# Seams of a two-stream transformer kernel: last chunks multiplied tile by tile, no context rows inside, and modulation pieces in places of their own

## The reference, cut to what matters

```python
def first_block(x, c, ...):
    c_act = jax.nn.silu(c)
    for l in range(DEPTH):                                  # 2
        mod = c_act @ w_ada[l] + b_ada[l]                   # 1024 -> 6 rows of 1024
        sh_m, sc_m, gt_m, sh_f, sc_f, gt_f = jnp.split(mod[:, None, :], N_MOD, axis=-1)
        h = rms_norm(x, g_pre_mix[l]) * (1.0 + sc_m) + sh_m
        y = token_mixer(h, w_in[l], ..., w_out[l], cos, sin)   # w_in 1024 x 3656, attention, w_out 1024 x 1024
        x = x + gt_m * rms_norm(y, g_post_mix[l])
        h = rms_norm(x, g_pre_ffn[l]) * (1.0 + sc_f) + sh_f
        y = conv_glu_ffn(h, w_up_act[l], w_up_lin[l], w_conv[l], b_conv[l], w_down[l])  # 2 x 2816 up, 2816 down
        x = x + gt_f * rms_norm(y, g_post_ffn[l])
    return x

def second_block(x, c, ctx, c_ctx, ...):
    for i in range(DEPTH):                                  # layer 0 even, layer 1 odd
        yc, yl = even_mixer(...) if i % 2 == 0 else odd_mixer(...)
        ...
        ff = peer(...)                                      # context and latents in layer 0, latents in layer 1
    return rmsnorm(hl, norm_f_g)

def peer(h, w_q, subkeys, u, v):                            # per token: 8 heads x 16 experts of 16384
    q = (xb @ w_q).reshape(PEER_BLOCK, PEER_HEADS, 2, PEER_DHALF)
    ...                                                     # top 16 of each half, then top 16 of 256 sums
    ue, ve = u[idx], v[idx]
    act = jax.nn.gelu(jnp.einsum('td,thkd->thk', xb, ue), approximate=False)
    return jnp.einsum('thk,thkd->td', g * act, ve)
```

## Time and profile before

| | us |
|---|---|
| median of three timed runs | 3843.72 |
| lowest and highest of them | 3842.69 and 3852.66 |
| the profiled execution's own time | 3842.15 |
| its span, first to last instruction | 3840.9 |
| TensorE busy in the span | 3050.1 (79%) |
| VectorE busy | 2455.0 (64%) |
| ScalarE, GpSimd busy | 784.2 (20%), 940.7 (24%) |
| moved by DMA | 1102.15 MB, mean 287 GB/s |

### The profile page before, as it was taken

The page is one execution under the profiler, slowest core; times in us unless marked ns, Lnnn a source line. Parts: engine busy times, 40 slices in busy tenths (PEclk is TensorE's granted clock), DMA queues, the critical chain, the costliest instruction groups (busy, mean ns, idle before and its releaser), DMA issues. The chain is left out here.

```text
span 3840.9 us, 28366 instructions
## 1 busy us (share of the span) xinstructions
PE 3050.1 (79%) x8769; PEld 1590.1 (41%) x8769; DVE 2455.0 (64%) x5374; ACT 784.2 (20%) x1876; POOL 940.7 (24%) x842
## 2 busy tenths in 40 slices
PE   6898797899786799787767777777897787777776
PEld 1354464675334377254344223322343462233322
DVE  3224556887677488646656999766514519999665
ACT  1102223232224433225211111100102211111000
POOL 0000001222221233222302344434100013444432
PEclk7999898999898899888879998999996799999999
DMA  6654234999795689966847999999632059999998
GB/s 236 201 178 167 93 114 169 343 356 354 301 356 199 230 349 406 373 248 212 306 154 294 391 388 389 392 422 422 257 138 103 21 206 367 386 389 376 422 421 348
DMA packets 194025, 1102.15 MB, mean 287 GB/s; under 512 B 22517, under 2 KB 22849, under 8 KB 95569
## 3 DMA queue, kind: packets, MB, share of 16 engines
q0 software_dynamic: 114512, 818.87, 54.1%
q1 hardware_dynamic: 78736, 280.90, 20.2%
q10 hardware_dynamic: 624, 0.57, 0.1%
HBM read 1099.18 MB, written 1.05 MB: 286 GB/s over the span
## 5 line engine op out<-in xcount | busy, mean ns | idle before, releaser
L2022 PE MATMUL PS<-AR 128*128 128x512 f32 x2464 | 1216.7, 639 | 400.7 <-DVE AR L2064 341.2
L2121 POOL DMA_INDIRECT AR<-in_uv,AR x768 | 866.1, 1128 | 1641.9 <-PE PS L2022 1142.8
L2069 DVE CUSTOM_DVE_ANT_0 AR<-AR 128x1024 f32<-128x1024 f32 x768 | 935.6, 1220 | 297.2 <-DMA AR<-in_uv,AR 296.7
L2022 PEld LDWEIGHTS PS<-AR 128*128 128x128 f32 x2464 | 476.1, 202 | 1103.3 <-DVE AR L2064 536.5
L694 PE MATMUL PS<-AR 128*128 128x512 f32 (+3 forms) x1304 | 565.3, 588 | 27.4 <-DMA AR<-in_w_in 14.7
L2034 ACT ACTIVATE AR<-AR 128x2 f32<-128x2 f32 x384 | 78.1, 203 | 1514.8 <-DVE AR L2069 1509.2
L694 PEld LDWEIGHTS PS<-AR 128*128 128x128 f32 x1304 | 250.5, 205 | 314.9 <-issue 269.5
L991 PE MATMUL PS<-AR 128*128 128x256 f32 x1408 | 327.2, 392 | 22.9 <-DMA AR<-in_w_up_act 11.9
L326 DVE SCALAR_TENSOR_TENSOR AR<-AR,CC 128x512 f32<-128x512 f32 x280 | 210.5, 752 | 208.5 <-DMA AR<-in_w_ada 130.7
L991 PEld LDWEIGHTS PS<-AR 128*128 128x128 f32 x1408 | 273.2, 196 | 85.0 <-issue 17.4
L1941 PE MATMUL PS<-AR 128*128 128x256 f32 x768 | 186.7, 406 | 26.7 <-DMA AR<-in_peer_w_q 19.6
(11 more groups left out here) (226 smaller groups left out, 2490.3 us busy)
## 6 DMA issues: line engine op xcount, KB each, us to landing
AR<-in_w_mod SPq DMA_DIRECT2D x96, 512.0 KB, 4.3
AR<-in_w_ada SPq DMA_DIRECT2D x96, 512.0 KB, 4.6
AR<-in_w_in SPq DMA_DIRECT2D x56, 512.0 KB, 4.0
AR<-in_peer_w_q SPq DMA_DIRECT2D x48, 512.0 KB, 3.3
AR<-in_w_up_act SPq DMA_DIRECT2D x44, 512.0 KB, 7.7
AR<-in_w_up_lin SPq DMA_DIRECT2D x44, 512.0 KB, 7.5
AR<-in_w_down SPq DMA_DIRECT2D x44, 512.0 KB, 9.6
AR<-in_even_w_in SPq DMA_DIRECT2D x24, 512.0 KB, 4.2
```

The costliest lines, as they stand in the source:

```text
L2022: ins = pe.eng.matmul(acc[i][hh], e.dg(x), e.buf(x)[:, 1024 + 512 * hh:1536 + 512 * hh], start=(x == e.on[False][i][0]), stop=(x == e.on[F ...
L2069: v.eng.tensor_tensor_reduce(e.buf(x)[:, 0:1024], e.buf(x)[:, 0:1024], norm2(e).H[e.tiles[x // 128]], 1.0, 0.0, ALU.mult, ALU.add, DT[x // ...
L2121: g.eng.indirect_dma_start(e.buf(x), None, D["uv"][e.l], bass.IndirectOffsetOnAxis(ap=idx_at(x // 16, x % 16, 1), axis=0)).then_inc(*land. ...
```

## The change

The last column block of a linear layer at a seam (w_out and w_down of layer 1, w_down of layer 0, the even mixer's output) is no longer multiplied chunk by chunk with tile 0 and tile 1 in turn: its four chunks are held in the ring, all of tile 0 is multiplied, then all of tile 1. The first column block after a norm (w_in of layer 1, the even mixer's input) is done in the same way. The epilogue (squares, root, gated add) is written for one tile at a time, and a dummy square root is put ahead of it. The shares at the seams (1.5 and 2.0) become 0, and the even mixer's shares are multiplied by 1.5. Modulation pieces of three sets (`ada0b`, `ada1a`, `ada1b`) go in halves of 256 KB into three places of their own instead of into the ring; in layer 1 they start four chunks later. Which context rows VectorE sums is moved by 8 to 11 rows. In the latents' query stages the top-k search starts at step 3 instead of 11, with four units instead of one, and the first no longer waits for the modulation rows, whose sums have moved out of its work area.

The diff, cut to its core:

```diff
@@ places and Mods @@
+        OWN_T = [T[:, a:a + 512] for a in (1536, 3072, 3584)]
+        OWN_BIG = [BIG[:, 5632 + 512 * i:6144 + 512 * i] for i in range(3)]
+        ACM = [area("acc")[:, 512 * i:512 * i + 512] for i in range(2)]
@@ Mods.sp @@
+                place, n = {}, len(self.own)
                 for j, hh, outs in self.halves:
                     r = 2 * j + hh
                     for kh in range(4):
-                        load(sp, ("raw", self.key, j, hh, kh), self.w[r, kh].rearrange("p (c n) -> p c n", c=2),
-                             2, 512, [("piece", self.key, j, hh, kh)])
+                        if n:
+                            for c in range(2):
+                                i = self.nth(j, hh, kh, c) % n
+                                sp.wait_ge(place.get(i, self.guard))
+                                sp.eng.dma_start(self.own[i], self.w[r, kh, :, 512 * c:512 * c + 512]).then_inc(
+                                    *land.landed(f"own{i}", "raw", self.key, j, hh, kh, c))
+                                place[i] = ("piece", self.key, j, hh, kh, c)
+                        else:
+                            load(sp, ...)
                         yield
@@ lin_pe @@
+                if c0 in whole:
+                    if k0 == 0:
+                        held = [(k, *chunk(pe, block(w, nk, c0, n, k, kk), kk, n, False)) for k in range(0, nk, kk)]
+                    if k0 // kk < len(tiles):
+                        t = tiles[k0 // kk]
+                        if t not in seen:
+                            prep.prep(pe, t)
+                            seen[t] = prep.turned(t)
+                        pe.wait_ge(seen.get(t))
+                        for ka, k, wt in held:
+                            pe.wait_ge(("raw", k))
+                            for kc in range(kk):
+                                ins = pe.eng.matmul(bks[k0 // kk][:, 0:n], lhs(ka + kc, t), wt[:, kc, :],
+                                                    start=(ka + kc == 0), stop=(ka + kc == nk - 1))
...
+                    yield
+                    continue
@@ lin @@
+                if c0 in whole:
+                    made = None
+                    if 0 <= k0 // kk - 2 < len(tiles):
+                        take(lane, tiles[k0 // kk - 2], c0, n)
@@ first block @@
+        HEAD, TAIL = ((), (0,)), ((), (512,))
-        CH, ROW, PACE, ATT = 0.45, 0.47, 0.8, (1.2, 0.5)
+        CH, ROW, PACE, ATT, SEAM = 0.45, 0.47, 0.8, (1.2, 0.5), 0.0
@@ first_pe, w_in (and the same loop condition in first_sp, first_act, first_dve, first_pool) @@
+            for i, _ in enumerate(lin_pe(pe, ("win", l), ..., ring=FIRST[l], whole=HEAD[l])):
+                if i >= 4 * len(HEAD[l]):
+                    pe.fill()
                 yield CH
@@ first_pe, w_out and the norm ahead of the FFN @@
-            yield 1.5
+            yield SEAM
             pe.run(mods_of["next", l])
             for t in range(2):
                 n2.prep(pe, t)
+            yield 1.0
             pe.wait_ge([n2.turned(t) for t in range(2)])
-            yield 1.0
@@ first_pe, w_down @@
             for f in range(22):
+                if f == 18:
+                    held = [(x, *chunk(pe, wd[:, x:x + 1, :], 1, 1024, False)) for x in range(18, 22)]
+                for x, k, wt in held if f in (18, 19) else ():
+                    pe.wait_ge(("raw", k), ("glu", l, x))
+                    down(x, k, wt, f - 18)
+                if f < 18:
+                    ...
                 yield CH
-            yield 2.0
+            yield SEAM
@@ first_act (first_dve and first_pool have add_dve and add_pool for tile f - 20 at the same f) @@
+            for f in range(22):
+                if f == 18:
+                    a.wait_ge(a.last)
+                    a.eng.activation(dum, dum, ACT.Sqrt).then_inc(*a.done())
+                if f >= 20:
+                    for hh in range(2):
+                        take_y(a, ("y", ("ffn", l)), f - 20, hh, ("mm", "y", ("ffn", l), f - 20))
+                    rms_y(a, l, 3, f - 20)
+                yield CH
+            yield SEAM
@@ even mixer, latent side @@
+                            whole=(0,) if side == "l" else ()):        # ein
+                            whole=(512,) if side == "l" else ()):      # eout
@@ who uses what @@
-                mods_of["first", 0] = ada("ada0b", 0, (2, 4, 3, 5), AF, {0: n1r, 1: n1r}, n1t)
+                mods_of["first", 0] = ada("ada0b", 0, (2, 4, 3, 5), AF, {0: n1r, 1: n1r}, n1t, OWN_T)
@@ (mods_of["first", 1] takes OWN_T too, mods_of["next", 0] takes OWN_BIG; more takes ACM for ACW) @@
-        ATTENTION, UPDOWN = range(98, 112), range(124, 188)
+        ATTENTION, UPDOWN = range(90, 104), range(114, 177)
-                          mods.finished() + [("sum", before, 255)], 11, 1)
-                  for l, mods, before in ((0, more, "c"), (1, mods_of["odd"], "l0"))]
+                          [("sum", before, 255)] + mods, 3, 4)
+                  for l, mods, before in ((0, [], "c"), (1, mods_of["odd"].finished(), "l0"))]
@@ both @@
-            merged(even(lane, "l"), beside, due)
+            merged((1.5 * share for share in even(lane, "l")), beside, due)
```

231 lines of the change are left out of this document (131 added, 100 removed).

## The result

The changed kernel takes 3898.16 us (median of four runs, 3894.65 to 3900.48); the kernel before took 3848.19 in the same session. The ratio is 1.0123, 95% interval 1.0102 to 1.0144: slower, where 3797 us had been predicted with a range up to 3842. The profiled execution took 3899.8 us (span 3898.5), 57.6 more than that of before.

What follows compares the result with a forecast made beforehand. It took TensorE to bound the kernel up to 1945 us, its idle time being what can be won, then VectorE and later DMA. Terms -47 - 24 + 36 - 8 + 5 + 3 - 12 = -47 gave 3797 us, 8-in-10 range 3750 to 3842.

Steps and rivals of the forecast that it cites:

- step 1: Four seams: rows taken out and epilogue by tile shorten them by 47 us together, bounds 30 to 60.
- step 2: Context rows moved: tail running alone 24 us less, even mixer 36 us more for 24 rows at 1.5 each.
- a sign of being wrong: Even mixer: the prediction would be wrong if it grew by more than 60 us.
- the other sign: Layer 0's FFN: the prediction would be wrong if weight waits grew there.
- the prediction's lower bound: Even mixer: 24 added rows cost 22 us, 0.93 each, if TensorE alone counts.
- any price above 3.4 us ends within 0.3% of no change: Even mixer's price per row, in the rival that rows are only moved: 3.9 us each, 3855 us; chance 0.11.
- step 3: Own places for modulation pieces: 8 us less from ring waits, 5 more from the first piece's wait at two starts.
- SP locked: Rival, 77 steps with pieces: VectorE a step behind holds SP's chunks, 1.6 us a step, 3928 us; chance 0.06.
- theory A: Follow-up theory, stages with pieces: own places tie SyncE's queue to VectorE, delaying weight chunks; costs 40 us.
- Query stages (+3): Latents' query stages: added top-k search lots meet modulation pieces, 3 us more (0 to 8).
- experts (-12): Two latent expert sets: search covers 112 rows, not 140, 6.2 us less in each, 12 less (8 to 16).
- rows only moved: Rival, even mixer: moved rows cost 3.9 us each, 94 rather than 36, giving 3855 us; chance 0.11.

Runs made afterwards that it cites:

- e10: Kernel before with only the context rows moved: no seam shares, even mixer's shares 1.5 times, row ranges as changed; 3850.16 us, 0.9998.
- e6: Changed kernel with modulation pieces back in the ring and context rows back where they were, so tile-wise products, query stages and experts remain; 3848.85 us, 1.0009.
- e8: Kernel before with only the query stages and experts as changed; 3830.05 us, 0.9955.
- e12: e6 with only w_down's four held chunks and the epilogues by tile left of the tile-wise part; 3842.43 us, 0.9983.
- e15: e12 with two of w_down's chunks held in place of four; 3836.87 us, 0.9977.
- e2: Changed kernel with the even mixer's shares taken once, not 1.5 times; 3918.22 us, 1.0189.
- e4: Changed kernel with context rows back in the seams, mixer's shares once and old row ranges, own places kept; 3890.31 us, 1.0115.
- e9: e6 without the tile-wise first block of layer 1's w_in, whose first four steps load pieces again; 3848.03 us, 0.9990.
- e7: Kernel before with only the modulation pieces in places of their own; 3878.54 us, 1.0090.
- e11: e8 with the even mixer's shares taken 1.5 times, seams untouched; 3832.62 us, 0.9965.
- e1: Changed kernel with the modulation pieces back in the ring of four places; 3863.76 us, 1.0038.
- e3: Changed kernel with pieces issued behind the weight chunk of two steps later in layer 0's FFN and layer 1's w_in; 3900.47 us, 1.0139.
- e5: Changed kernel with seven own places in place of three for the modulation pieces of layer 0's FFN; 3881.66 us, 1.0089.
- e13: Kernel before with rows moved, query stages and experts as changed, and six units of the context's top-k search in its query stage, not five; 3839.32 us, 0.9973.
- e14: As e13, but five units, and four search steps beside each context row in place of three; 3852.14 us, 1.0008.
- e16: Changed kernel with six units of the context's top-k search in its query stage, not five; 3893.10 us, 1.0123.

## Why the prediction was wrong

The sum said 47 us less, and the kernel takes 50 more. Four steps failed. Places of their own were put at 3 less (-8 and +5) and cost 33. The rows in the even mixer were put at 36 and came with 56. The tile-wise products were put at nothing outside the seams and cost some 19 with their seams counted in. Layer 1's attention had no term and grew by 17. (These overlap: the 19 hold some of the mixer's and the attention's growth, less the 6 that the tile-wise part wins in the seams.)

**The seams (-47, step 1): nearly right in size, wrong in what earns it.** 41.9 us were won. But e10 wins 35.8 of them by the shares alone; the tile-wise products and epilogues add 6. And the sum costed these at nothing elsewhere. They cost some 19 us in all (e6 against e8), of which one place is shown and one is likely. With four chunks held, w_down 1 takes 87.0 us (e12), with two 83.3 (e15), and with none and the rows as before 82.0 to 83.7: a hold of four in a ring of four leaves no place to load ahead. In the changed kernel w_down 1 grew by more, 10.6 us; 5.4 are the three waits for held chunks, and 4.2 are TensorE's wait for VectorE ahead of the stage (1.1 before), which the moved rows bring without any held chunk (5.5 in e10):

```profile
1554.05 69.07 PE L1061 MATMUL PS<-AR 128*128 128x512 f32 x148 [5.28 <-DVE AR L1295]
```

The likely place is the even mixer, where a block is held at the start and one at the end: with 45 or 46 rows in it, it takes 253.5 to 260.8 us in the four kernels that hold them (e2, e4, e6, e9) and 248.4 to 252.3 in the five that don't (before, e7, e8, e12, e15). For the rest of the 19 no single run stands.

**The rows (-24 and +36, step 2): the mixer's term was too small, the tail's too large.** The mixer grew by 55.9 us, just short of the 60 that I had named as a sign of being wrong; the other sign, longer weight waits in layer 0's FFN, did come (10.4 to 25.3 us for w_up_act). 20 rows came in, not 24; by e2 a row costs 2.07 us, in e10 2.6, in e11 3.2, where I took 1.5. The place where it failed is "but in its attention TensorE is idle a quarter of the time ... and a row more lengthens both": I saw the chain and still took a price near TensorE's own. TensorE's part of the price was right: its products for rows in the mixer went from 52.1 to 73.7 us, 21.6 more where the prediction's lower bound has 22, and its busy time from 212.4 to 233.7. The other 35 us are idle time of TensorE (36.6 before, 71.3 after), which the sum put at 14. The largest waits that came with it (before, mixer; then changed, mixer):

```profile
PE PS L516 <- DVE MOD L339: 7.5, 1, 7.5
```

```profile
PE PS L2109 <- ACT AR L2136: 17.1, 5, 4.3
PE PS L540 <- DVE MOD L363: 14.1, 2, 10.4
```

Of before, the view has no wait for a row's diagonal matrix; changed, TensorE waits 17.1 us for those that ScalarE makes (L2136), all of it in the attention, and e10 has 16.7. So half of the added idle time is the rows' own chain: a row's products come up in TensorE's order before ScalarE is through with its weight. It isn't the whole price, since e11 has only 4.9 us of this wait and its rows are no cheaper. Where ScalarE's time goes is seen in the changed mixer's attention (timeline):

```profile
1802.85 0.69 ACT L1684 ACTIVATE AR<-PS,SM 128x512 f32<-128x512 f32 x1
...
1804.02 1.28 ACT L2121 ACT_TABLE_LOAD   x1 [0.39 <-DVE AR L2156]
1805.31 0.20 ACT L2121 ACTIVATE AR<-AR 128x2 f32<-128x2 f32 x1
1805.53 1.28 ACT L1684 ACT_TABLE_LOAD   x1
1806.83 0.69 ACT L1684 ACTIVATE AR<-PS,SM 128x512 f32<-128x512 f32 x1
```

A row pair's gelu of 0.20 us between two exponentials of the softmax costs 1.28 + 0.20 + 1.28, 2.8 us with the gaps. Of before and changed, the groups of these loads in the mixer's attention:

```profile
L2034 ACT ACT_TABLE_LOAD x9 | 11.5, 1283 | 16.1 <-DVE AR L2069 16.1
```

```profile
L2121 ACT ACT_TABLE_LOAD x13 | 16.7, 1283 | 15.4 <-DVE AR L2156 15.4
```

The softmax's own loads went from 9 to 13 as well: 8 loads more, 10.3 us of a chain that grew by 33. The count goes with the rows: 13 and 13 in e10 and e11 too, 9 and 9 in e2. TensorE's idle time in that part rose from 29 to 52 us. That the loads are what a row costs there was not tried by itself. The Trainium skill (ScalarE: Activation LUTs, What ACT_TABLE_LOAD costs) has the load at about 1283 ns, which agrees, and a drain behind it, which again does not show: 1804.02 + 1.28 and the next activation at 1805.31.

The tail was to lose 9.1 rows at 2.65, 24 us; it lost 5 rows and gave 9 us, part of the stretch being fixed (e11: 12.3 us with no row left). Added to this, the seams' row price and the mixer's: the rows' whole move is worth nothing (e10, 3850 against 3846). The rival's line "any price above 3.4 us ends within 0.3% of no change" is a slip: by the prediction's own numbers it is 3.0 (3797 and 24 rows at 1.5 more reach 3832).

**Own places (-8 and +5, step 3): the step that failed by the most.** 3 less in the sum, 33 to 34 more in e7 and e1. "I take a third of the gain" had no row behind it. What I wrote of the order, that chunk s + 1 stands behind VectorE's piece of step s - 1, is what SyncE's waits show (107.6 for 40.2), and the rival "SP locked" named it. I gave it 0.06 because VectorE stays a row or more ahead of TensorE, which was no protection: VectorE itself waited for pieces (25.1 us, 5.2 before), and a piece that lands late is read late and frees its place late. It came at 33/77 = 0.43 us a step, not at 1.6 and under the 0.7 from which I said it decides: alone it would have given 3797 + 36 = 3833. What neither I nor theory A had: the ring lends pieces up to four whole places, the own places only one and a half, and with a landing of some 6 us that is too little for VectorE in layer 0's FFN, whatever the order (e3, e5). For the stretch to w_out 0 (some 8 us longer in every kernel with three places) and for w_in 1 more places were not tried. The first piece's stall was 9.7 us in FFN 0, where I had 2.5 for it: until both tiles are transposed no piece is issued, and SyncE's next chunk is behind. The transposes end at 658.0; SyncE's queue and then TensorE:

```profile
658.91 0.86 SPq L294 DMA_DIRECT2D AR<-in_w_ada  x2
659.82 0.43 SPq L246 DMA_DIRECT2D AR<-in_w_up_act  x1
```

```profile
659.11 5.12 PE L1048 MATMUL PS<-AR 128*128 128x256 f32 x16 [1.08 <-DVE AR L1973]
673.95 6.24 PE L1048 MATMUL PS<-AR 128*128 128x256 f32 x16 [9.71 <-DMA AR<-in_w_up_act]
```

(Changed: the second chunk is issued at 659.8 behind the first pieces, TensorE is through with the first at 664.2, and starts the second at 673.9, when it has landed.) Seven places don't help this: e5 has 9.6 us there.

**Layer 1's attention (no term, +17).** A context row carries three steps of VectorE's top-k search with it, and that work ends with the 97th row. Before, row 97 fell at 1171 us, the very end of w_in; only one step of the search lay in the attention. With eight rows fewer done by then 31 steps, 8.8 us of VectorE, lie inside it, in e10 as in the changed kernel. Taking the search forward gives 7 to 8 us of the attention back (e13, e14, e16: 119.7, 118.2, and 125.2 for 132.7) but hardly any of the total: 5 us in e16, inside the noise. Some 3 to 4 us of the 11 in e10 have no run. The changed kernel's other 10 us have no clear cause: in e6 only 3 steps of the search lie in the attention and it takes 127.0, without the held block of w_in (e9) 118.4, but e4 takes 120.9 with it. I had costed "the row ranges" and not asked which other work is counted in rows.

**Query stages (+3) and experts (-12): right for the experts.** The first query stage changed by 0 and the two sets by -14.5; e8 alone measures -15. The odd mixer with the second queries grew by 5.3 (4.0 in e8), for which the sum had nothing but the 3; its cause was not looked for.

**Put together**, in ratios to before: places +0.90%, rows -0.02%, experts -0.45%, tile-wise +0.54% (e6 less e8). That is +0.97% or 37 us; measured are +1.23%, which is 47 us of 3848 (the two medians are 50 apart). The 10 us between are within what the intervals leave open, or the parts hinder each other (e1 is 0.31% above rows, tile-wise and experts added). Among the rivals none came true alone: SP locked at a quarter of its price, rows only moved at 2.1 to 3.2 us and not 3.9, and a cost of the held chunks and the search which no case had.

Faster than both kernels is e8: 3830 us, 0.9955. None of the others, with rows or held chunks added to it, beats it (e11, e13, e15); e11, 3 us behind, is level with it to the measurement.

## What to carry to other kernels

Before a side stream gets places of its own, compare them with what it could borrow from the shared ring: here three half places cost 33 us, and seven in one stage gave back what they had cost there and no more. Count them in loads in flight against the landing time, and count the first load's guard. An idle seam filled with another stream's steps isn't lost time: emptying it moves the work to a place with a price of its own, and moves everything that is tied to those steps (a search, a table switch) across the stages behind. When chunks are held for a second pass, a ring with no place left over turns the hold into waits for loads (three of 1.8 us here).

## What the runs showed of the hardware

- A gelu of 0.20 us between two softmax exponentials costs two table loads of 1.28 us each: 13 + 13 loads in 161 us, for the gelus of 18 pairs of rows. No other pause shows at such a load: the activation ahead ends at 1805.51, the load starts at 1805.53, and the exponential at 1806.83.
- SyncE's queue, moved two steps, cut TensorE's waits for weights in layer 0's FFN from 30 to 8 us, but the stage took 241.9 us, within the 241.3 to 247.7 of all kernels with three places: the wait came back through VectorE's late pieces as 18.5 us for a row's diagonal.
- Loads of 256 KB served layer 0's FFN as well as those of 512 KB (226.4 us in e5, 224.9 in e1) once there were seven places for them.
- The same program can differ by 18 us in one stage from one execution to the next (FFN 0: 238.6 us in e9, 220.3 in e12).
